# Identity transposes in TensorE's waits, and three loads moved, in a two-layer hybrid encoder

## What is computed

```python
def reference(x, c, ...):
    cond = silu(c)
    for l in range(2):
        sh1, sc1, g1, sh2, sc2, g2 = split(cond @ w_ada[l] + b_ada[l], 6)
        u = x * (1 + sc1) + sh1
        y = even_mixer(u, ...) if l % 2 == 0 else odd_mixer(u, w_qkv, rel_bias, w_o)
        x = layer_norm(ALPHA * x + (1 + g1) * y, ln_g[l, 0], ln_b[l, 0])
        u = x * (1 + sc2) + sh2
        y = conv_ffn(u, w_up[l], conv_w[l], conv_b[l], w_down[l])
        x = layer_norm(ALPHA * x + (1 + g2) * y, ln_g[l, 1], ln_b[l, 1])
    return x
```

## Time and profile before

| | |
|---|---|
| runs | 2354.05, 2356.56, 2356.84 us |
| median | 2356.56 us |
| profiled execution | 2356.47 us |
| its span, first to last instruction | 2354.7 us |
| busy: PE, DVE, ACT | 2213.7 (94%), 1720.8 (73%), 1011.1 us (43%) |
| moved by transfers | 612.62 MB, 260 GB/s in the mean |
| mean granted clock of PE | 0.976 of 2.4 GHz |

### The profile page before, as it was taken

One profiled execution on the slowest core, in us unless ns is written; L12 is line 12 of the kernel. 1 busy time (PEld: TensorE's weight loads), 2 busy tenths in 40 slices (PEclk: granted clock), 3 DMA queues, 4 the chain that ended last, 5 costly groups with the idle time before them and its releaser, 6 DMA issues. The chain is left out here.

```text
span 2354.7 us, 27597 instructions
## 1 busy us (share of the span) xinstructions
PE 2213.7 (94%) x11043; PEld 1866.2 (79%) x11043; DVE 1720.8 (73%) x1674; ACT 1011.1 (43%) x1008; POOL 8.7 (0%) x19
## 2 busy tenths in 40 slices
PE   4799997889999999999989999998999999999996
PEld 3587776778888888888777888886888888888885
DVE  6798889858977778788767667675599755665555
ACT  2345343444443444453345445435544434544432
POOL 1000000000000000000000000000000000000000
PEclk9899998989999999999989999998999999999998
DMA  9999688958878888879949778774588656566553
GB/s 372 323 407 346 240 300 313 320 171 293 274 274 301 305 281 280 280 265 313 341 142 339 250 259 283 259 262 157 175 302 285 224 191 204 182 197 193 189 191 121
DMA packets 392225, 612.62 MB, mean 260 GB/s; under 512 B 21113, under 2 KB 205073, under 8 KB 390562
## 3 DMA queue, kind: packets, MB, share of 16 engines
q1 hardware_dynamic: 391442, 610.52, 74.5%
q0 software_dynamic: 448, 0.25, 0.0%
q10 hardware_dynamic: 208, 0.10, 0.0%
HBM read 608.70 MB, written 2.10 MB: 259 GB/s over the span
## 5 line engine op out<-in xcount | busy, mean ns | idle before, releaser
L875 DVE TENSOR_TENSOR w_lo<-w_raw,w_hi 128x2048 fp32r<-128x2048 f32 x380 | 847.9, 2233 | 418.7 <-ACT w_hi L547 351.6
L547 ACT ACTIVATE w_hi<-w_raw 128x2048 fp32r<-128x2048 f32 x380 | 710.3, 1870 | 872.5 <-PE banks L1325 519.0
L1384 PE MATMUL banks<-u_hl,w_hi 128*128 128x512 f32 x2368 | 576.6, 392 | 8.7 <-DVE g_sum L1051 6.9
L1384 PEld LDWEIGHTS banks<-u_hl,w_hi 128*128 128x128 f32 x2368 | 432.7, 188 | 96.0 <-DVE g_sum L1051 9.4
L1323 PE MATMUL banks<-w_hi,u_hl 128*128 128x512 f32 x896 | 367.4, 410 | 24.6 <-DVE u_hl L942 24.4
L1325 PE MATMUL banks<-w_hi,u_hl 128*128 128x512 f32 x896 | 356.7, 398 | 0.0
L1392 PEld LDWEIGHTS banks<-u_hl,w_lo 128*128 128x128 f32 x2368 | 308.6, 191 | 14.5
L1392 PE MATMUL banks<-u_hl,w_lo 128*128 128x256 f32 x2368 | 313.1, 283 | 0.0
L1323 PE MATMUL banks<-w_hi,hid_hi 128*128 128x512 f32 x688 | 269.6, 392 | 0.0
L1325 PE MATMUL banks<-w_hi,hid_lo 128*128 128x512 f32 x688 | 267.8, 389 | 0.0
L886 DVE SCALAR_TENSOR_TENSOR ada_acc<-ada_w,silu_c,ada_acc 128x1024 f32<-128x1024 f32 x194 | 248.2, 1280 | 20.0 <-DMA ada_w<-in_w_ada 13.3
(11 more groups left out here) (222 smaller groups left out, 1464.0 us busy)
## 6 DMA issues: line engine op xcount, KB each, us to landing
ada_w<-in_w_ada SPq DMA_DIRECT2D x352, 512.0 KB, 6.7
w_raw<-in_w_up SPq DMA_DIRECT2D x344, 512.0 KB, 4.8
w_raw<-in_w_down SPq DMA_DIRECT2D x152, 512.0 KB, 4.8
w_raw<-in_w_qkv SPq DMA_DIRECT2D x96, 512.0 KB, 4.9
w_raw<-in_w_in_ab SPq DMA_DIRECT2D x64, 512.0 KB, 8.0
ada_w_more<-in_w_ada SPq DMA_DIRECT2D x32, 512.0 KB, 10.2
w_raw<-in_w_out_ab SPq DMA_DIRECT2D x32, 512.0 KB, 5.2
w_raw<-in_w_o SPq DMA_DIRECT2D x32, 512.0 KB, 4.9
```

The lines of the kernel that those rows point to most:

```text
L547: nc.scalar.activation(whi[:, u % HL_SLOTS, 0:width], raw[:, u % RAW_SLOTS, 0:width], ACT.Copy).then_inc(w_hi, 1)
L875: nc.vector.tensor_tensor(wlo[:, u % HL_SLOTS, 0:width], raw[:, u % RAW_SLOTS, 0:width], whi[:, u % HL_SLOTS, 0:width].bitcast(f32), ALU.s ...
L1384: ins = nc.tensor.matmul(bank[banks[s] + i][:, :], tile(whi, k, s, i), uhl[:, kt].rearrange("p a s -> p (a s)"), start=first and k == 0, s ...
```

## The change

Four things change.

1. PE gets a new operation, `warm(n)`: n transposes of the identity matrix into the first 128 columns of a bank that nobody reads. It is called with 100 before the sum of pair 0, once ACT has taken the second x piece, and with 26 behind it, ahead of unit 0; with 64 before the sum of pair 1, again once the x piece is out, and with 18 behind it, ahead of unit 3; with 80 before the sum of pair 9, into that sum's own bank; and at each of the three LayerNorms with 46 before the first two pieces' transposes and 12 behind them. In all 462.
2. In `mlp` the gate bias is loaded behind five chunks of up_a and not behind one.
3. The rows of pair 17, the last of layer 0, are spread over 10 units and not 12; they end, and their sum stands, two units earlier.
4. `toeplitz` is issued from ACT's queue, behind the high part of unit 6 of the attention (u = 4), with the wait for the fourth `ln_affine`. On SP that wait and the table are gone; the gate bias stands behind unit 8.

```diff
+WARM_SUMS = {0: 100, 1: 64, 9: 80}
+WARM_U = {0: 26, 2: 18}
+WARM_LN, WARM_LN_U = 46, 12
...
-    fill(17, first + 78, [1, 2, 1] * 4)
+    fill(17, first + 78, [2, 2, 2, 2, 2, 2, 1, 1, 1, 1])
...
             def mlp(layer, uses):
-                phase((layer, "up_a"), 0, 1)
+                phase((layer, "up_a"), 0, 5)
                 gate_load(layer, 5, uses)
-                phase((layer, "up_a"), 1, 10)
+                phase((layer, "up_a"), 5, 10)
...
-                if v == 7:
-                    sp.wait_ge(sem("ln_affine"), 8)
-                    rb = A["rel_bias"]
-                    sp.dma_start(toep[:, :, :], bass.AP(rb.tensor, REL - 127, [[1, P], [2 * REL + 1, AH], [1, S]])
-                                 ).then_inc(sem("toep_in"), 16)
+                if v == 8:
                     gate_load(1, 2, 12)
...
             for u in range(ATT_UNITS):
                 hi_unit(ATT_U + u + 2)
+                if u == 4:
+                    act.wait_ge(sem("ln_affine"), 8)
+                    rb = A["rel_bias"]
+                    act.dma_start(toep[:, :, :], bass.AP(rb.tensor, REL - 127, [[1, P], [2 * REL + 1, AH], [1, S]])
+                                  ).then_inc(sem("toep_in"), 16)
...
+            def warm(n, to=bank[7]):
+
+                for _ in range(n):
+                    nc.tensor.transpose(to[:, 0:P], ident, ident)
+
             def ada_sum(m, k):
 
                 acc = acc_of(m)
+                if m in (0, 1):
+                    pe.wait_ge(sem("xT_out"), 2 * m + 2)
+                    warm(WARM_SUMS[m])
+                if m == LATE_PAIRS[1]:
+                    pe.wait_ge(a_out, SUM_NO[m, k] + 1)
+                    warm(WARM_SUMS[m], T[1])
...
+                if u == 0:
+                    warm(WARM_U[0])
                 unit(u, [(k, 4 * j + k) for k in range(4)], (uhi, ulo), first, last, bank[b:b + 2], after)
...
                 beside(u)
+                if u == 2:
+                    warm(WARM_U[2])
 
             def ln_T(s, pieces):
+                if pieces == (0, 1):
+                    warm(WARM_LN)
                 for v in pieces:
...
+                if pieces == (0, 1):
+                    warm(WARM_LN_U)
```

## The result

The changed kernel takes **2339.4 us** (median of 4 runs, 2338.22 to 2343.65) against 2356.64 beside it: ratio 0.9929, interval 0.9917 to 0.9942, a gain of 17.2 us. I had said 2336 (2327 to 2349), faster.

What follows compares the result with a forecast made beforehand. PE was taken as the bound, so time could come only from its idle time and half-clock work. The terms 1.7 + 1.9 + 4.5 + 2.0 + 0.5 + 1.9 + 7.6 = 20.1 us, from 2356.47, gave 2336 (range 2327 to 2349).

Steps and rivals of the forecast that it cites:

- first sum: Front: 100 transposes raise the clock, so the first modulation sum takes 1.84 us in place of 3.57; 1.7 us.
- second sum, unit 3: Front: 64 and 18 transposes bring full clock to the second sum and unit 3; 1.9 of 3.8 us, kept.
- LayerNorms: Three LayerNorms: transposes hold the clock through part of each wait; 1.5 us each, 4.5 in all.
- sum of pair 9: Wait before pair 9's sum: 80 transposes hold the clock; 2.0 us, from 0 to 4.5.
- gate bias: up_a: loads behind the gate bias are issued earlier, so DVE waits less before pair 9; 0.5 us, 0 to 1.5.
- last rows: End of layer 0: a modulation row no longer stands between PE's end and DVE's last residual; 1.9 us.
- bias table: Attention: unit 8 and its row load before the table, removing PE's 5.15 us wait and half-clock work; 7.6 us, 5 to 7.75.
- rival (b): Remaining gaps: the clock falls in nearly all of them, leaving 10.3 us of gain, 2346; chance 0.20.
- Rival (a): Remaining gaps: the clock holds through all of them, every term full, 2327; chance 0.15.
- (c): All added transposes: they don't hold or raise the clock; 11 us lost against 10.0 gained, 2357, no change; chance 0.08.
- (d): All added transposes: each waits for the one before, lasting its full 0.27 us; 47 lost against 10, 2393; chance 0.05.
- The row that I had held against (c): At 328.76: eight transposes, then 4.22 us idle, clock still 1.00 at 335.1, 6.3 us from the last ordinary matmul.

Runs made afterwards that it cites:

- moves_only: Changed kernel with all added transposes at 0, the table, gate bias and last rows still moved: 2346.62 us against 2355.78 for the kernel before, ratio 0.9965.
- warm_only: Kernel before with the 462 transposes alone, none of the moves: 2349.15 us against 2355.78, ratio 0.9971.
- gate_back: Changed kernel with the gate bias loaded behind the first chunk of up_a again: 2339.28 us beside 2339.22 for the changed kernel.
- front_off: Changed kernel without the front's four groups of transposes (100, 26, 64, 18): 2343.40 us, ratio 0.9938, beside 2339.22 for the changed kernel.
- more_warm: Changed kernel with longer groups: 64 and 34 transposes at each LayerNorm, 94 before pair 9's sum, 14 before pair 8's: 2334.81 us, ratio 0.9913.
- combined_front: Changed kernel with the edits of act_order and more_warm, pair 17's sum in the LayerNorm's wait, 90 transposes before the second sum, 46 before unit 0: 2331.35 us.
- act_order: Changed kernel with ACT's first two activation pieces ahead of unit 1's high part, and pieces 4 to 7 one unit later: 2340.03 us, ratio 0.9929.
- table_on_sp: Kernel before with the table still on SP's queue but behind unit 9's loads, gate bias behind unit 8: 2350.09 us against 2355.78, ratio 0.9974.
- table_only: Kernel before with the table's load moved to ACT's queue and the gate bias behind unit 8, nothing else: 2349.28 us against 2355.78, ratio 0.9974.

## Why the prediction held, and where it didn't

The sum said 20.1 us and 17.2 came. Term by term, the size being the stage's step in kernels with the edit, less that in kernels without it:

| term | predicted | measured |
|---|---|---|
| first sum | 1.7 | 0 |
| second sum, unit 3 | 1.9 | 1.6 at unit 4, 0.85 kept |
| LayerNorms | 4.5 | 2.0 + 0.6 + 0.9 = 3.5 |
| sum of pair 9 | 2.0 | 3.0 |
| gate bias | 0.5 | 0 |
| last rows | 1.9 | 2.03 |
| bias table | 7.6 | 7.9 |
| all | 20.1 | 17.3 |

The first LayerNorm and pair 9 are means of seven kernels with the changed kernel's groups there (-1.6 and -2.6) against four without (+0.4 and +0.3), with single values from -0.8 to -3.2 and from +0.1 to -5.7; that the column adds up so near to the 17.2 of the medians is better than such means deserve. Luck helped the forecast too: four terms (both of the front, the LayerNorms, the gate) were 4.3 us too high together, and pair 9, the rows and the table gave 1.4 back. The 0.6 of the second LayerNorm is the changed kernel's step of 2.64 less the 2.03 of `moves_only`; in `warm_only` this stage came out 0.25 later. There the last rows stand where they stood, PE is idle for 4.25 us and not 1.96 before the real transposes, and the clock fell in that wait, at 1175.92. So in these profiles the transposes of this LayerNorm earn something only together with the moved rows. The 0.9 of the third is 0.74 in the mean of those seven, and 0.2 late in the four.

**First sum: the step failed.** "DVE carries this on" read the wrong engine. DVE was busy, but what starts it is unit 0's activations, and these stood on ACT behind two high parts that waited for weights. I had read PE and DVE at the front and not ACT. The sum did become 1.95 us, the sign that I had named, and it was worth nothing: a sign that an edit works is not yet a sign that it pays. Unit 0 even starts later, by 0.26 to 2.44 us, in all six kernels with these transposes and the old order of ACT. What goes with it in the traces is the fetching of instructions. In all nine kernels with the front's transposes one 16 KB packet of instructions, 0.93 to 1.12 us long, passes a transfer engine between 27.5 and 29.8 us; in the other five the first of that size comes at 53.7 or later. ACT's first high part, which waits for weights, starts 0.4 to 2.1 us behind the end of DVE's last row of pair 0 in the nine, and within 0.2 us of it in the five. That the packet delays the weights is argued from this alone; no run tests it.

**Second sum: "so the gain is kept" failed.** PE is dense from unit 4 on, but unit 15's high part hangs on ACT's wait for the result of pair 2, and that on rows whose loads come no sooner; DVE's wait for a row grew as PE got ahead of it (3.28 us before, 4.12 in the changed kernel, for the row at 116). I had named this as what would make me most wrong, and gave it no price in the sum; it cost 0.75 us, with or without the two kernels with slower transfers. How much is left, 0.85 or 1.5, is less sure.

**LayerNorms: right mechanism, too large.** My 1.5 each were half of the half-clock work. In the changed kernel's profile the clock held through the LayerNorm in all three, but the eight transposes gave only 0.45 of the 0.88 us that they became shorter: 1182.30 to 1187.57 in the earlier trace rows is 5.27 us, 1180.78 to 1185.60 is 4.82, since DVE's normalisation and ACT's activations run beside half of them. And it fell behind the last 2.42 us of idleness, for 3.4 us of unit work, at every LayerNorm. Other profiles of the same code are worse: at the second LayerNorm of `gate_back` and `front_off` the clock fell at 1177.72 and 1182.19, early in the 12 transposes behind the real ones, and was low for 6.8 us, though PE had been idle for only 1.96 us before. That was rival (b)'s half of the truth: what the changed kernel leaves to be had is the 1.6 us per LayerNorm of `more_warm`. Rival (a), 2327, needs those gaps closed; `combined_front`, which closes most of them, came to 2331.35.

**Pair 9** came out within its range. What I had feared there, that PE comes sooner than DVE and the gap widens, was seen at the front instead, in `act_order`.

**Last rows: right number for a wrong reason.** In `moves_only` y_gated starts at 1179.67 and PE's last matmul ends at 1179.63 (1186.62 less its idle time of 6.99): the sign that I had named. But it didn't begin sooner: against units 190 to 199 it starts when it did before (1175.36 + 4.31 = 1179.67). PE ended 1.70 us later, because the pair's sum came with its rows. "a modulation row, which the change moves away" left out that a sum follows the rows. The gain was made two units on, where the sum no longer stands: 2.05 us. Free of that sum the rows are worth 1.1 more.

**Table: right**, and a little above the end of its range: 7.9 for 5.15 + 2.6, as the clock no longer falls at all there. PE has no wait of 0.3 us or more in the attention's first twelve units, and the rows behind unit 9 made DVE wait 0.27 and 0.50 us. `table_on_sp` shows that the order was the reason and not the queue. "It costs nothing" on ACT held as well: ACT's wait ended at 1217.0, its next high part waited for PE until 1221.11.

**The rivals.** (c) and (d) are settled by the 100 transposes at the front: up to 22.3 a new one starts every 0.21 us (24 in 5 us, half clock, though the first stretch is shown as 1.00 as in the kernel before), from 23 on every 0.104 (67 in 7 us).

```profile
17.30:22.30 5.00, 5.00 (x24) 5.00 (x25) 4.58 (x5) 0.00 (x0) 0.00 (x0) 1.00 1.05 407
23.00:30.00 7.00, 7.00 (x67) 7.00 (x66) 6.43 (x6) 0.00 (x0) 0.00 (x0) 1.00 1.06 409
```

So they don't wait for each other (no 0.27 at full clock), and the clock rose while PE did nothing but transposes, and held through 34 more of them in `more_warm`. Here the Trainium skill ("TensorE: Matmul & The Clock Gate", Part 4: PE-mode transpose), by which full clock doesn't engage for transposes, and the trace differ; the trace decides (the skill's times there are for bfloat16, and these transposes are float32). The row that I had held against (c) says less than I made of it: the clock was still 1.00 at 335.1, but it fell at 335.18.

## What to carry to other kernels

A faster step is worth what the next engine in line does with it: before you price one, read the queue of every engine between it and the next bound, in its own order, and see what stands ahead of the dependent instruction there. When instructions are moved, count all that follow them by rule (here a sum behind its last row), and ask at each new place whether that engine has time to spare. Filling a wait with work to hold the clock pays in full only if it is filled to its end (3.5 us at three LayerNorms as they were filled here, 1.6 more at each of the last two when filled to the end), and a wait that is made longer by a gain elsewhere needs a longer filling.

## What I had not expected of the hardware

The same 2 MB table, in the same pieces, took very different times to land. Issued from ACT's queue while SP's goes on with weights (the changed kernel):

```profile
DMA to landing us min/median/max: 22.9/22.9/22.9
```

From SP's queue in `table_on_sp`, with weights before and behind it:

```profile
DMA to landing us min/median/max: 13.3/13.3/13.3
```

It was 9.5 us in the kernel before and 23.1 in `table_only`. A queue beside another busy one was the slower way for this transfer by 10 us; it cost nothing, as DVE first reads the table at 1245.8, 5.9 us after it landed. And a clock that had been low from the start of the program came up at 22.64, behind 5.4 us of transposes back to back and with no ordinary matmul of the units before it.
